# Norms 0, 2 and 3 of a hybrid decoder trunk: an earlier residual add on VectorE and a new order on ScalarE

## The chip, the cores and the metric

The kernel runs on one core of one Trainium2 chip. The metric is the device time of one execution in microseconds (us), the median of three runs. The engines are TensorE (PE, with its weight loads PEld), VectorE (DVE), ScalarE (ACT), GpSimd (POOL) and SyncE (SP), which issues the loads of the weights.

## The reference, cut to what matters

Two layers; each has four sublayers, and each sublayer ends in a layer norm of a residual sum. Everything is fp32.

```python
for l in range(DEPTH):
    x = layer_norm(ALPHA * x + 0.5 * swiglu(x, ffn1_w_in[l], ffn1_w_out[l]), ln1_g[l], ln1_b[l])
    x = layer_norm(ALPHA * x + mix, ln2_g[l], ln2_b[l])               # mix: RG-LRU, GLA, conformer
    x = layer_norm(ALPHA * x + memory_cross_attn(...), ln3_g[l], ln3_b[l])
    x = layer_norm(ALPHA * x + 0.5 * swiglu(x, ffn2_w_in[l], ffn2_w_out[l]), ln4_g[l], ln4_b[l])

def layer_norm(x, g, b):
    mu = jnp.mean(xf, axis=-1, keepdims=True)
    var = jnp.mean(jnp.square(xf - mu), axis=-1, keepdims=True)
    y = (xf - mu) * lax.rsqrt(var + EPS)
    return (y * g + b).astype(x.dtype)
```

The norms are numbered 0 to 3 in the kernel.

## The kernel before, in words

`x` lies in SBUF as 128 partitions by 8 feature tiles (`k` or `m`) by 512 positions. Every product is made of three passes: an operand is split into a high part (fp32r) and a low part, and TensorE adds high by high, high by low and low by high. Weights come as "slots" through a ring of four buffers `raw`; ScalarE copies a slot into one of two buffers `w_hi` (`w_hi_of`, L1272), GpSimd subtracts to get `w_lo` (`split`, L567), and TensorE multiplies. `w_hi_of(n)` waits until slot n-2 has been multiplied, since it overwrites that slot's buffer.

Norms 0, 2 and 3 work by halves of the positions, `h` = 0 (positions 0 to 255) and `h` = 1. For one of them the work goes as follows; `next_s` is the first slot of the next stage, `a` the first half, `b` the second:

- TensorE finishes the last output tile (norm 0, 3) or the last two (norm 2) for half `a`, then for half `b`. DVE adds the residual of half `a` (`half_added`, L1778), and later that of half `b` (`added_b`, which waits for TensorE's slot and calls `half_added` once for norm 0 and 3, twice for norm 2).
- TensorE sums over the features with a matrix of 1/1024 (L809: `stats_first`, `stats_rest`). ACT squares the mean (`square_of_mean`, L1312), DVE makes the variance (`variance`, L1784 and L1786), ACT its reciprocal root (`root`, L1316), and DVE refines the root (`scale`, L1792 to L1796).
- DVE centres `x` two tiles at a time (`centered_pair`, L1820), scales them (`normed_pair`, L1826) and in half 1, for `k` = 4 and 6, also applies gain and bias (`affine_pair`, two instructions L1832, SBUF to SBUF). For all other pairs ACT applies gain and bias (`affines`, L1322). ACT copies each pair to its high part (`copied`, L1366), and GpSimd makes its low part (`split_x`, L575).
- Meanwhile TensorE does not wait for the norm: `raw_pair` (L751, L753, L756) multiplies slots `next_s` and `next_s`+1 with the un-normed sums (made by ACT at L1294 and DVE at L1752), and a correction is applied afterwards (`sums_of` on ACT, L1371 to L1373). The sum over half `b` for the statistics (`stats_rest(…, 1)`) stands inside the first of these products, behind `k` = 5 (norm 0, 3) or `k` = 7 (norm 2). Then `second_pair` (L777, L783, L790) multiplies slot `next_s`+2 with the normed `x`, half by half: it waits for `w_hi`, for `sums_of(0)`, for each pair's high part, for `w_lo` and for each pair's low part.

All queues run in the order in which the code issues; there is no scheduler. GpSimd's order at a norm (`after_norm`) is: split of slots `next_s` and `next_s`+1, four `split_x` of half 0, split of slot `next_s`+2, four `split_x` of half 1, split of slot `next_s`+3. Norm 1 is not by halves, and norm 3 of the last layer takes other functions (`scaled_by_halves`) and keeps its order, so five norms are touched: norm 0, 2, 3 of layer 0 and norm 0, 2 of layer 1.

Of the kernel before, what the change touches and what calls it, by code (L numbers as in the profile page):

```python
# [65 lines left out]
def slot_width(s):  # L66

    if S_OUT[0] <= s < S_MIX or s >= S_OUT[1]:
        return FT // 2 * P
    if S_MIX + V_SLOT <= s < S_MIX + V_SLOT + 2:  # L70
        return 4 * W_B
    return KT * P
# [32 lines left out]
def group(layer, n, h):  # L105
    return layer * GROUPS + G_BASE[n] + h + 1
# [7 lines left out]
def later(layer, n):  # L114

    return n in RAW_NORMS and (layer, n) != (LAYERS - 1, 3)
# [19 lines left out]
def raw_bank(n, j, h):  # L136
    return 2 * (1 - j if n == 2 else j) + h
# [18 lines left out]
def x_count(layer, n, k, h=0):  # L156
    return KT + layer * XS + X_BASE[n] + h * KT + k + 1
# [47 lines left out]
def raw_count(n):  # L205

    return 16 * sum(pieces(i % SLOTS) for i in range(n % RAW, n + 1, RAW))
# [22 lines left out]
def hybrid_decoder(nc, x_in, mem_in, consts_in, vecs_in, mats_in, w_in1, w_out1, w_in2, w_out2,  # L230
                   w_mix, w_v, w_mixout, w_kv, w_q, w_o, out):
    ctx = ExitStack()
    with ctx:
# [77 lines left out]
        def tokens_in(n, h):  # L311
            return HALVES[h] if BY_HALVES[n] else slice(0, SEQ)

        def mean_of(n, h):
            return psum[:, 6 + h, HALVES[0]] if BY_HALVES[n] else bank(6)
# [7 lines left out]
        def first_root_of(n, h):  # L323
            return psum[:, 4 + h, HALVES[1]] if BY_HALVES[n] else bank(4)
# [931 lines left out]
        def _(act):  # L1256
# [8 lines left out]
            def w_hi_of(n):  # L1265

                if n >= SPLIT:
                    act.wait_ge(slot_multiplied, n - SPLIT + 1)
                if n < TOTAL:
                    act.wait_ge(raw_loaded[n % RAW], raw_count(n))  # L1270
                    width = slot_width(n % SLOTS)
                    A(w_hi[:, n % SPLIT, 0:width], raw[:, n % RAW, 0:width],  # L1272
                      ACT.Copy).then_inc(w_hi_made, 1)
# [33 lines left out]
            def silu_table():  # L1307
                A(small[:, 46:47], small[:, 47:48], ACT.Silu)

            def square_of_mean(layer, n, h):  # L1310
                act.wait_ge(stats_ready, group(layer, n, h))
                A(var[:, tokens_in(n, h)], mean_of(n, h), ACT.Square).then_inc(mean_squared, 1)  # L1312

            def root(layer, n, h):
                act.wait_ge(var_ready, group(layer, n, h))
                A(first_root_of(n, h), var[:, tokens_in(n, h)],  # L1316
                  ACT.Abs_reciprocal_sqrt).then_inc(root_ready, 1)

            def affine(layer, n, k, cols):
                act.wait_ge(y_centered, x_count(layer, n, k, 1 if cols.start else 0) - KT)  # L1320
                c = V_LN + 16 * n + k
                return A(x[:, k, cols], x[:, k, cols], ACT.Identity, bias=vec(c + 8), scale=vec(c))  # L1322
# [33 lines left out]
            def scaled_later(layer, n, next_s, square_b, to):  # L1356

                hi = NORMED[n][0]

                def affines(h, k):  # L1360
                    affine(layer, n, k, HALVES[h])
                    affine(layer, n, k + 1, HALVES[h])

                def copied(h, k):
                    cols = HALVES[h]
                    A(hi[:, k:k + 2, cols], x[:, k:k + 2, cols], ACT.Copy).then_inc(x_hi_made, 2)  # L1366

                def sums_of(j):
                    act.wait_ge(slot_multiplied, next_s + j + 1)
                    o = to(j)  # L1370
                    A(sums[:, 2 * j:2 * j + 2], psum[:, raw_bank(n, j, 1), HALF:HALF + 2], ACT.Copy)  # L1371
                    A(o[:, HALVES[0]], psum[:, raw_bank(n, j, 0), HALVES[0]], ACT.Copy)
                    A(o[:, HALVES[1]], psum[:, raw_bank(n, j, 1), HALVES[0]],  # L1373
                      ACT.Copy).then_inc(raw_sums_read, 1)

                square_of_mean(layer, n, 0)
                if n == 2:
                    w_hi_of(next_s)
                root(layer, n, 0)
                if n != 2:  # L1380
                    w_hi_of(next_s)
                affines(0, 0)
                affines(0, 2)
                square_b()
                w_hi_of(next_s + 1)
                if n != 2:
                    act.wait_ge(slot_multiplied, next_s)
                act.drain()
                copied(0, 0)
                copied(0, 2)  # L1390
                square_of_mean(layer, n, 1)
                affines(0, 4)
                root(layer, n, 1)
                affines(0, 6)
                act.drain()
                copied(0, 4)
                copied(0, 6)
                for k in range(0, KT, 2):
                    if k < 4:
                        affines(1, k)  # L1400
                        act.drain()
                    else:
                        act.wait_ge(y_centered, x_count(layer, n, k + 1, 1) - KT)
                    copied(1, k)
                    if k == 0:
                        sums_of(0)
                        w_hi_of(next_s + 2)
                    if k == 4:
                        w_hi_of(next_s + 3)
                sums_of(1)  # L1410
                silu_table()
# [311 lines left out]
        def _(dve):  # L1723
# [19 lines left out]
            def raw_lo(layer, n, m, h, cols):  # L1743

                c = V_LN + 16 * n
                z_hi, z_lo = RAW_Z[n]
                dve.wait_ge(raw_hi_made, raw_part(layer, n, m, h))
                if m == 0:
                    V.tensor_tensor(z_lo[:, :, SEQ:ROW],
                                    vecs[:, c:c + 2 * KT].rearrange("p (w k) -> p k w", w=2),  # L1750
                                    z_hi[:, :, SEQ:ROW].bitcast(F32), ALU.subtract)
                V.scalar_tensor_tensor(z_lo[:, m, cols], x[:, m, cols], vec(c + m),  # L1752
                                       z_hi[:, m, cols].bitcast(F32), ALU.mult,
                                       ALU.subtract).then_inc(raw_lo_made, 1)
# [26 lines left out]
            def variance(layer, n, h, eps):  # L1781

                v = var[:, tokens_in(n, h)]
                V.tensor_tensor(v, square_mean_of(n, h), v, ALU.subtract)  # L1784
                dve.drain()
                V.tensor_scalar(v, v, 0.0, eps, ALU.max, ALU.add).then_inc(var_ready, 1)  # L1786

            def scale(layer, n, h):

                v, r0 = var[:, tokens_in(n, h)], first_root_of(n, h)  # L1790
                dve.wait_ge(root_ready, group(layer, n, h))
                V.scalar_tensor_tensor(v, v, -0.5, r0, ALU.mult, ALU.mult)  # L1792
                dve.drain()
                V.tensor_tensor(v, v, r0, ALU.mult)
                dve.drain()
                V.scalar_tensor_tensor(scale_of(n, h), v, 1.5, r0, ALU.add, ALU.mult)  # L1796
# [20 lines left out]
            def centered_pair(n, h, k):  # L1817
                cols = HALVES[h]
                m = mean_of(n, h).rearrange("p (a s) -> p a s", a=1).to_broadcast([P, 2, HALF])
                V.tensor_tensor(x[:, k:k + 2, cols], x[:, k:k + 2, cols], m, ALU.subtract)  # L1820
# [15 lines left out]
            def norm_by_halves(layer, n, eps, added_b):  # L1836

                for h in range(2):
                    if h:
                        added_b()  # L1840
                    if later(layer, n):
                        for m in range(WHOLE[n], KT):
                            raw_lo(layer, n, m, h, HALVES[h])
                    dve.wait_ge(mean_squared, group(layer, n, h))
                    variance(layer, n, h, eps)
                    centered_pair(n, h, 0)
                    centered_pair(n, h, 2)
                    scale(layer, n, h)
                    normed_pair(n, h, 0).then_inc(y_centered, 2)
                    normed_pair(n, h, 2).then_inc(y_centered, 2)  # L1850
                    for k in range(4, KT, 2):
                        centered_pair(n, h, k)
                        last = normed_pair(n, h, k)
                        if h and later(layer, n):
                            last = affine_pair(n, h, k)
                        last.then_inc(y_centered, 2)
# [464 lines left out]
```

## Time and profile before

| what | value |
|---|---|
| runs (us) | 2215.99, 2216.14, 2215.76; median 2215.99 |
| profiled execution | 2216.65 us, span 2214.9 us |
| PE busy | 2171.3 us (98%) |
| PEld busy | 1814.8 us (82%) |
| DVE busy | 1119.5 us (51%) |
| ACT busy | 824.0 us (37%) |
| POOL busy | 990.5 us (45%) |
| mean granted TensorE clock | 0.997 |

Busy times are of the profiled execution; its own time is 1.75 us above its span, and 0.66 us above the median. Matmuls are pipelined, so a row of PE overlaps the next one: one 256-column matmul is listed with about 0.28 us, and the next starts 0.12 us after it. Below, a time such as 383.60 is us from the start of the span. A row of the timeline gives start, length, engine, line, operation, output and inputs with shape, the count of merged instructions, and in brackets the idle time of the engine before it and what ended that.

### The profile page before, as it was taken

Reading aid. Unit: us, or ns where it says so; the run is one execution under the profiler, and the core shown is the slowest. Engines: PE = TensorE matmul, PEld = TensorE weight load, DVE = VectorE, ACT = ScalarE, POOL = GpSimd, SP = SyncE. Lnnn points to the kernel's source line nnn. Section 1 sums busy time; section 2 is a strip of 40 time slices with the busy share of each in tenths; the row PEclk is TensorE's granted clock in tenths of the full one; section 3 lists DMA queues with packets and bytes.
Section 4 is the critical chain, followed back from the end, with each engine's and each line's share of the span. In section 5 each row is a group of like instructions: output and inputs, shape, how many; then the busy total and the mean of one; then the engine's idle time right before and its main releaser. Section 6 shows DMA issues by size and latency. Waiting matters only on the chain. (4 is left out here: it accounts for less than half of the span.)

```text
span 2214.9 us, 26968 instructions
## 1 busy us (share of the span) xinstructions
PE 2171.3 (98%) x11052; PEld 1814.8 (82%) x11052; DVE 1119.5 (51%) x1222; ACT 824.0 (37%) x1148; POOL 990.5 (45%) x408
## 2 busy tenths in 40 slices
PE   8999999999999999999999999999999999999997
PEld 7888889788778888888888888898786888888886
DVE  4433235987746733323454333369877376333234
ACT  3322224836444522222353222257355344222223
POOL 3444444436443544444354444454265335444442
PEclk9999999999999999999999999999999999999999
DMA  5333322333332233332233333223243222333321
GB/s 179 96 95 95 114 100 62 89 103 105 107 93 67 77 95 96 96 120 92 74 105 95 95 99 117 89 67 86 90 121 113 77 67 80 101 96 95 114 94 49
DMA packets 96043, 210.91 MB, mean 95 GB/s; under 512 B 39344, under 2 KB 52016, under 8 KB 95664
## 3 DMA queue, kind: packets, MB, share of 16 engines
q1 hardware_dynamic: 94944, 208.19, 30.4%
q8 instruction: 87, 1.43, 0.3%
q10 hardware_dynamic: 976, 1.00, 0.1%
q14 instruction: 36, 0.29, 0.0%
HBM read 207.06 MB, written 2.10 MB: 94 GB/s over the span
## 5 line engine op out<-in xcount | busy, mean ns | idle before, releaser
L567 POOL TENSOR_TENSOR w_lo<-raw,w_hi 128x1024 fp32r<-128x1024 f32 (+2 forms) x358 | 930.9, 2602 | 1197.0 <-ACT w_hi L1272 1196.9
L1272 ACT ACTIVATE w_hi<-raw 128x1024 fp32r<-128x1024 f32 (+2 forms) x358 | 401.6, 1122 | 1217.8 <-PE psum L647 1141.1
L641 PE MATMUL psum<-acts_hi,w_hi 128*128 128x512 f32 x1744 | 685.1, 393 | 3.4 <-ACT tmp L1648 3.0
L644 PE MATMUL psum<-acts_lo,w_hi 128*128 128x512 f32 x1744 | 679.8, 390 | 0.0
L647 PE MATMUL psum<-acts_hi,w_lo 128*128 128x512 f32 x1744 | 430.8, 389 | 0.0
L641 PEld LDWEIGHTS psum<-acts_hi,w_hi 128*128 128x128 f32 x1744 | 328.0, 188 | 76.5 <-issue 3.9
L644 PEld LDWEIGHTS psum<-acts_lo,w_hi 128*128 128x128 f32 x1744 | 328.0, 188 | 69.7 <-issue 2.4
L647 PEld LDWEIGHTS psum<-acts_hi,w_lo 128*128 128x128 f32 x1744 | 327.4, 188 | 68.0
L1885 DVE TENSOR_TENSOR work<-work,psum 128x512 f32<-128x512 f32 x85 | 58.5, 688 | 548.8 <-PE psum L647 542.0
L641 PE MATMUL psum<-h_hi,w_hi 128*128 128x512 f32 x616 | 239.6, 389 | 0.0
L644 PE MATMUL psum<-h_lo,w_hi 128*128 128x512 f32 x616 | 239.6, 389 | 0.0
L1890 DVE TENSOR_TENSOR h_lo<-work,h_hi 128x512 fp32r<-128x512 f32 x88 | 231.2, 2628 | 6.6
L1766 DVE SCALAR_TENSOR_TENSOR x<-x,psum 128x512 f32<-128x512 f32 x56 | 38.4, 686 | 283.9 <-PE psum L647 283.4
L647 PE MATMUL psum<-h_hi,w_lo 128*128 128x512 f32 x616 | 148.7, 389 | 0.0
L1773 DVE TENSOR_TENSOR work<-work 128x512 f32<-128x512 f32 x54 | 138.2, 2559 | 14.5 <-ACT work L1302 12.7
L644 PEld LDWEIGHTS psum<-h_lo,w_hi 128*128 128x128 f32 x616 | 115.6, 188 | 24.0
L641 PEld LDWEIGHTS psum<-h_hi,w_hi 128*128 128x128 f32 x616 | 115.6, 188 | 24.0
L647 PEld LDWEIGHTS psum<-h_hi,w_lo 128*128 128x128 f32 x616 | 115.6, 188 | 24.0
L1969 DVE SCALAR_TENSOR_TENSOR psum<-tmp,vecs,psum 128x512 f32<-128x512 f32 x116 | 87.6, 755 | 9.2 <-issue 0.4
L1302 ACT ACTIVATE work<-x 128x512 f32<-128x512 f32 (+1 forms) x72 | 41.1, 571 | 61.4 <-DVE x L1778 41.2
L1322 ACT ACTIVATE x<-x,vecs 128x256 f32<-128x256 f32 (+1 forms) x92 | 53.5, 630 | 19.5 <-DVE x L1826 14.4
L1771 DVE TENSOR_TENSOR work<-work,x 128x512 f32<-128x512 f32 x54 | 52.1, 964 | 5.3 <-issue 0.4
(300 smaller groups left out, 2484.6 us busy)
## 6 DMA issues: line engine op xcount, KB each, us to landing
raw<-w_in SPq DMA_DIRECT2D x176, 512.0 KB, 3.6
raw<-w_out SPq DMA_DIRECT2D x64, 704.0 KB, 4.0
raw<-w_kv SPq DMA_DIRECT2D x32, 512.0 KB, 3.6
raw<-w_mix SPq DMA_DIRECT2D x26, 512.0 KB, 3.6
raw<-w_q SPq DMA_DIRECT2D x16, 512.0 KB, 3.6
raw<-w_o SPq DMA_DIRECT2D x16, 512.0 KB, 3.6
raw<-w_v SPq DMA_DIRECT2D x4, 768.0 KB, 4.2
raw<-w_mix SPq DMA_DIRECT2D x24, 128.0 KB, 3.3
```

Of the source, the lines that this page charges most:

```text
L567: nc.gpsimd.tensor_tensor(w_lo[:, n % SPLIT, 0:width], raw[:, n % RAW, 0:width], w_hi[:, n % SPLIT, 0:width].bitcast(F32), ALU.subtract).t ...
L641: nc.tensor.matmul(o, hi, b_hi, start=start and k == 0, stop=False)
L644: nc.tensor.matmul(o, hi, b_lo, start=False, stop=False)
L647: last = nc.tensor.matmul(o, weight(r, k)[1], operand(k)[0], start=False, stop=stop and k == n - 1)
L1272: A(w_hi[:, n % SPLIT, 0:width], raw[:, n % RAW, 0:width], ACT.Copy).then_inc(w_hi_made, 1)
L1302: A(zsq(m)[:, cols], x[:, m, cols], ACT.Square).then_inc(z_squared, 1)
L1322: return A(x[:, k, cols], x[:, k, cols], ACT.Identity, bias=vec(c + 8), scale=vec(c))
L1771: V.tensor_tensor(zsum, zsum, x[:, m, :], ALU.add)
L1773: V.tensor_tensor(zsqsum, zsqsum, zsq(m), ALU.add).then_inc(z_summed, 1)
L1885: V.tensor_tensor(h, work[:, i % 2, :], bank(hidden_bank(layer, f, i, 1)), ALU.mult).then_inc(h_made, 1)
L1890: V.tensor_tensor(lo, h, hi.bitcast(F32), ALU.subtract).then_inc(h_split, 1)
L1969: V.scalar_tensor_tensor(total, u_pad[:, t, j:j + SEQ], w, total, ALU.mult, ALU.add)
```

## The change

In `norm_by_halves` (DVE) `added_b` moves from the start of half 1 into half 0: in norm 2 ahead of the pair `k` = 4, in norms 0 and 3 ahead of the pair `k` = 6. In `scaled_later` (ACT) `square_of_mean` of half 1 moves ahead of the first two copies of half 0, `root` of half 1 ahead of `affines(0, 4)`, and `w_hi_of(next_s + 2)` from behind `sums_of(0)` to ahead of the loop over half 1.

```diff
@@ scaled_later, ScalarE
                 square_b()
                 w_hi_of(next_s + 1)
+                square_of_mean(layer, n, 1)
                 if n != 2:
                     act.wait_ge(slot_multiplied, next_s)
                 act.drain()
                 copied(0, 0)
                 copied(0, 2)
-                square_of_mean(layer, n, 1)
+                root(layer, n, 1)
                 affines(0, 4)
-                root(layer, n, 1)
                 affines(0, 6)
                 act.drain()
                 copied(0, 4)
                 copied(0, 6)
+                w_hi_of(next_s + 2)
                 for k in range(0, KT, 2):
...
                     if k == 0:
                         sums_of(0)
-                        w_hi_of(next_s + 2)
@@ norm_by_halves, VectorE
                 for h in range(2):
-                    if h:
+                    if h and not later(layer, n):
                         added_b()
...
                     for k in range(4, KT, 2):
+                        if h == 0 and later(layer, n) and k == (4 if n == 2 else 6):
+                            added_b()
                         centered_pair(n, h, k)
```

VectorE's queue in norm 2 of layer 0, from the scaling of the first two pairs of half 0, before:

```order
L1826 TENSOR_TENSOR x<-x,psum 128x2x256 x2
L1820 TENSOR_TENSOR x<-x,psum 128x2x256
L1826 TENSOR_TENSOR x<-x,psum 128x2x256
L1820 TENSOR_TENSOR x<-x,psum 128x2x256
L1826 TENSOR_TENSOR x<-x,psum 128x2x256
L1778 SCALAR_TENSOR_TENSOR x<-x,psum 128x256 x2
L1752 SCALAR_TENSOR_TENSOR z_lo<-x,vecs,z_hi 128x256 x2
L1784 TENSOR_TENSOR var<-psum,var 128x256
```

And the same stretch after the change:

```order
L1826 TENSOR_TENSOR x<-x,psum 128x2x256 x2
L1778 SCALAR_TENSOR_TENSOR x<-x,psum 128x256 x2
L1820 TENSOR_TENSOR x<-x,psum 128x2x256
L1826 TENSOR_TENSOR x<-x,psum 128x2x256
L1820 TENSOR_TENSOR x<-x,psum 128x2x256
L1826 TENSOR_TENSOR x<-x,psum 128x2x256
L1752 SCALAR_TENSOR_TENSOR z_lo<-x,vecs,z_hi 128x256 x2
L1784 TENSOR_TENSOR var<-psum,var 128x256
```

The two residual adds (L1778) stand four instructions earlier; in norms 0 and 3 the one add stands two earlier, ahead of the last L1820 and L1826 of half 0.

ScalarE's queue in norm 0 of layer 0, as the difference from the copy of slot `next_s`+1 on (L1272 is a weight copy, L1312 the squared mean, L1316 the root, L1322 gain and bias, L1366 a copy to the high part):

```order
 L1272 ACTIVATE w_hi<-raw 128x1024
+L1312 ACTIVATE var<-psum 128x256
 L1366 ACTIVATE x_hi<-x 128x2x256 x2
-L1312 ACTIVATE var<-psum 128x256
-L1322 ACTIVATE x<-x,vecs 128x256 x2
-L1316 ACTIVATE psum<-var 128x256
-L1322 ACTIVATE x<-x,vecs 128x256 x2
+L1316 ACTIVATE psum<-var 128x256
+L1322 ACTIVATE x<-x,vecs 128x256 x4
 L1366 ACTIVATE x_hi<-x 128x2x256 x2
+L1272 ACTIVATE w_hi<-raw 128x1024
 L1322 ACTIVATE x<-x,vecs 128x256 x2
```

The squared mean now stands ahead of two copies, the root ahead of all four gains of `k` = 4 to 7, and the third weight copy ahead of half 1's first gains. TensorE's queue, GpSimd's and SyncE's are as before.

## Rows read from the trace of the kernel before

**Rows 1.** Who TensorE waited for: us in total, times, longest us (whole run)
```profile
PE psum L809 <- DVE x L1778: 2.7, 3, 1.1
PE psum L790 <- POOL x_lo L575: 2.6, 3, 0.9
```

**Rows 2.** TensorE's timeline, norm 0 of layer 0: its last two waits
```profile
389.49 0.50 PE L777 MATMUL psum<-x_hi,w_hi 128*128 128x256 f32 x2 [0.24 <-ACT x_hi L1366]
...
392.59 0.50 PE L790 MATMUL psum<-x_lo,w_hi 128*128 128x256 f32 x2 [0.92 <-POOL x_lo L575]
```

**Rows 3.** TensorE's timeline, norm 2 of layer 0
```profile
732.27 1.12 PE L1227 MATMUL psum<-q_hi,w_lo 128*128 128x256 f32 x8
...
737.48 1.13 PE L809 MATMUL psum<-x,consts 128*128 128x256 f32 x4 [1.05 <-DVE x L1778]
...
748.97 1.22 PE L777 MATMUL psum<-acts_hi,w_hi 128*128 128x256 f32 x8 [0.78 <-ACT w_hi L1272]
...
753.62 0.50 PE L777 MATMUL psum<-acts_hi,w_hi 128*128 128x256 f32 x2 [0.24 <-ACT acts_hi L1366]
...
756.52 0.50 PE L790 MATMUL psum<-acts_lo,w_hi 128*128 128x256 f32 x2 [0.73 <-POOL acts_lo L575]
```

**Rows 4.** TensorE's timeline, norm 0 of layer 0: last slot of the stage
```profile
371.44 1.67 PE L888 MATMUL psum<-h_hi,w_lo 128*128 128x256 f32 x11
```

**Rows 5.** VectorE's timeline, norm 0 of layer 0
```profile
373.25 0.41 DVE L1778 SCALAR_TENSOR_TENSOR x<-x,psum 128x256 f32<-128x256 f32 x1
...
377.51 0.58 DVE L1786 TENSOR_SCALAR var<-var 128x256 f32<-128x256 f32 x1
...
383.60 0.73 DVE L1832 TENSOR_SCALAR x<-x,vecs 128x256 f32<-128x256 f32 x2
...
385.78 2.93 DVE L1832 TENSOR_SCALAR x<-x,vecs 128x256 f32<-128x256 f32 x2
```

**Rows 6.** ScalarE's timeline, norm 0 of layer 0
```profile
376.61 0.36 ACT L1312 ACTIVATE var<-psum 128x256 f32<-128x256 f32 x1
...
378.12 0.39 ACT L1316 ACTIVATE psum<-var 128x256 f32<-128x256 f32 x1 [0.17 <-DVE var L1786]
...
379.60 1.15 ACT L1366 ACTIVATE x_hi<-x 128x512 fp32r<-128x512 f32 x2
...
383.69 1.07 ACT L1272 ACTIVATE w_hi<-raw 128x1024 fp32r<-128x1024 f32 x1
...
388.80 0.63 ACT L1366 ACTIVATE x_hi<-x 128x512 fp32r<-128x512 f32 x1 [0.89 <-DVE x L1832]
```

**Rows 7.** GpSimd's timeline, norm 0 of layer 0
```profile
375.55 2.39 POOL L567 TENSOR_TENSOR w_lo<-raw,w_hi 128x1024 fp32r<-128x1024 f32 x1 [3.69 <-ACT w_hi L1272]
377.90 5.11 POOL L575 TENSOR_TENSOR x_lo<-x,x_hi 128x512 fp32r<-128x512 f32 x4
384.85 2.41 POOL L567 TENSOR_TENSOR w_lo<-raw,w_hi 128x1024 fp32r<-128x1024 f32 x1 [1.83 <-ACT w_hi L1272]
387.21 5.33 POOL L575 TENSOR_TENSOR x_lo<-x,x_hi 128x512 fp32r<-128x512 f32 x4
```

**Rows 8.** Timelines of VectorE, ScalarE and GpSimd, norm 2 of layer 0
```profile
732.57 1.47 DVE L1826 TENSOR_TENSOR x<-x,psum 128x512 f32<-128x512 f32 x2
...
741.63 0.61 DVE L1786 TENSOR_SCALAR var<-var 128x256 f32<-128x256 f32 x1
...
733.29 2.09 ACT L1322 ACTIVATE x<-x,vecs 128x256 f32<-128x256 f32 x4 [2.27 <-DVE x L1826]
737.13 0.42 ACT L1302 ACTIVATE work<-x 128x256 f32<-128x256 f32 x1 [1.75 <-DVE x L1778]
...
739.67 2.42 POOL L567 TENSOR_TENSOR w_lo<-raw,w_hi 128x1024 fp32r<-128x1024 f32 x1 [6.43 <-ACT w_hi L1272]
```

**Rows 9.** L1752 on VectorE over the run: duration ns min/median/max
```profile
L1752 DVE SCALAR_TENSOR_TENSOR z_lo<-x,vecs,z_hi x20: 484/739/2877, 701.9 to 1836.8; 128x512 fp32r<-128x512 f32 x12, 128x256 fp32r<-128x256 f32 x8
```

**Rows 10.** VectorE's timeline in the mixer of layer 0: its slack against TensorE
```profile
474.91 1.38 DVE L2024 COPY_PREDICATED work<-consts,psum 128x1024 f32<-128x1024 uint32 x1 [2.54 <-PE psum L988]
```

## The prediction

> **What bounds the kernel now.** I read the page's busy times first: TensorE is busy 98% of the span at a granted clock of 0.997, so the time can fall only where TensorE waits, and rises only where it waits more. The list of TensorE's waits comes next. The waits of the touched norms are small: three times for the residual add at the statistics (two of them, 1.05 us each, in norm 2), three times for GpSimd's low part of `x` in norms 0 and 3 [rows 1, 3]. Then the timelines of the engines in one norm 0 and one norm 2; layer 1 and norm 3 repeat them within 0.3 us. In norm 0 TensorE waits 0.24 us for the high part of the last pair and 0.92 us for its low part [rows 2]. In norm 2 it waits 1.05 us at the statistics, 0.78 us for the third weight copy, and 0.24 and 0.73 us for the last pair [rows 3]. All of it together, over five norms, is under 10 us; it is the most that there is to win.
>
> The reader should see one more thing, the length of VectorE's L1832 (gain and bias). The pair of `k` = 4 takes 0.73 us while GpSimd is idle; the pair of `k` = 6 takes 2.93 us while GpSimd works without a gap [rows 5, 7]. Its two instructions end about 0.15 us after an instruction of GpSimd each: the split ends at 387.26, the first low part at about 388.55, and the pair ends at 388.71. L1786 does the same: reached at 377.51, it ends at 378.09, 0.15 us after GpSimd's split (377.94). So such an instruction waits for the GpSimd instruction that is running, and the next for the one after it. The Trainium skill says this as a rule (SBUF — State Buffer, Who interferes with whom): a `tensor_scalar` in a 2-port mode and a GpSimd instruction exclude each other for a whole instruction. The trace agrees (0.73 against 2.93 us).
>
> **Norms 0 and 3 (three of them).** The times are of norm 0 in layer 0.
> - The earlier add. TensorE's last slot ends at 371.44 + 1.67 = 373.11 [rows 4], and the add started at 373.25 [rows 5]. It can win 0.14 us at most; I take 0.08. VectorE stands still for it from 371.9, then does `k` = 6 of half 0; that was idle time before, and ACT wants that pair only at 378. Cost nothing.
> - Squared mean. The statistics stand at a fixed place in TensorE's queue, done at 376.1. ACT squares at 376.17, not 376.61 [rows 6]. VectorE reaches L1786 about 0.5 us earlier, but GpSimd's split runs till 377.94 - 0.08 [rows 7], so the variance ends at 378.01 instead of 378.09, and the root starts at 378.04 instead of 378.12. The new place of `square_of_mean` buys 0.08 us.
> - Root ahead of four gains. Four L1322 take 2.1 us behind the root where two did. The copies of `k` = 4 and 6 start at 380.51 instead of 379.60, 0.9 us later. GpSimd's third low part starts at 381.22; with 1.25 to 1.3 us each (5.11 for four) the fourth ends at 383.78, not 383.01.
> - Third weight copy. It follows the copies, at 381.57 to 382.64 instead of from 383.69: 2.1 us earlier. GpSimd's split runs at 383.73 to 386.13 instead of 384.85 to 387.26, 1.1 us earlier, and its idle time of 1.83 us [rows 7] is gone.
> - What is late next. The pair `k` = 4 of half 1 lay in that idle time. Now VectorE reaches it at 383.55, GpSimd is busy till 383.78, the first instruction ends at 383.93, and the second waits for the whole split, till 386.28 (before 384.33). The pair `k` = 6 comes 1.44 us later (385.78 - 384.33, about), at 387.72; its instructions end behind the second and third low part, at 388.87 and 390.15, instead of 388.71. ACT's copy takes 0.09 + 0.63 us, so TensorE gets the last pair at 390.93 instead of 389.49. From there to the last low part it has 14 matmuls at 0.12 us and a restart, 2.01 us: 392.94 instead of 392.59. GpSimd has its low part by 392.3; that wait is gone. Per norm **+0.35 us**.
>
> Bounds: were VectorE never held, the last pair would stay at 389.49 and TensorE would end at 391.50, -1.1 us. If VectorE reached `k` = 4 just after GpSimd began the split (0.2 us decide), both its instructions wait, the pair ends at 387.75, and `k` = 6 at 390.65: +0.85 us. A further low part of 1.3 us is the far end, +1.3 us in all; more is not to be had, because GpSimd itself starves without the last pair and lets VectorE in. I take +0.35, since 383.55 lies before 383.73. Sum of three: +1.05.
>
> **Norm 2 (two of them).** The times are of layer 0.
> - The earlier add wins much here: TensorE's slots are done at 733.39 [rows 3], VectorE is free at 733.96 (rows 8: 732.57 + 1.47, overlapping a little). The statistics follow TensorE's product with no wait at 736.17 instead of 737.48, -1.31 us for TensorE at that point.
> - ACT's squares start right behind its four gains (733.29 + 2.09), at 735.28 instead of 737.13, and with them the second weight copy and GpSimd's split, which started at 739.67 [rows 8]: -1.85 us, so 737.82 to 740.24.
> - VectorE does its two L1752 behind `k` = 6 now: the second starts at 733.96 + 2 x 0.33 + 2 x 1.36 + 0.4 = 737.74. It reads two operands from SBUF, and the long ones of this line (2877 ns against 739) [rows 9] wait, as I read it, for GpSimd too. It is 0.08 us ahead of GpSimd. If it is first, GpSimd starts at 738.2, ends at 740.60, the variance ends at 740.75 instead of 742.24 (741.63 + 0.61 in rows 8): -1.49 us.
> - From there the chain of norm 0: `k` = 4 is reached 5.51 us behind the variance (378.09 to 383.60), at 746.26; ACT's copies let GpSimd's fourth low part end at 746.52 and the split at 748.87; VectorE ends `k` = 4 at 749.02, `k` = 6 at 752.90. TensorE gets the last pair at 753.68 (before 753.62) and ends at 755.69 instead of 756.52. The waits at the statistics and for the weight copy go, but most of it comes back as a longer wait for the last pair. Per norm **-0.83 us**.
>
> Bounds: with the affine pair never held, GpSimd's chain sets the end, at about 754.0 (-2.5 us), and without any hold of the variance either, -3.6 us. On the other side stands the second rival below, +0.07 us. Sum of two: -1.66.
>
> **Downstream.** VectorE leaves norm 0 at 390.15 instead of 388.71. Two L2079 follow that waited for GpSimd before and will wait less, and in the mixer VectorE still has 2.54 us in hand where TensorE keeps it waiting [rows 10]. I count nothing.
>
> **Sum.** 2216.65 (the profiled execution: span 2214.90 and 1.75 around it) + 1.05 - 1.66 = 2216.04. The profiled run was 0.66 above the median, so **2215.4** against 2215.99.
>
> **Rivals.** Within 0.2% (4.4 us) a measurement of this kernel can't tell from no change.
> - *L1752 loses in norm 2.* GpSimd starts first by a few hundredths; the second L1752 waits till 740.24, the variance then stands behind the first low part and ends at 741.65. The last pair comes at 754.58, TensorE ends at 756.59, +0.07. For it: the margin is 0.08 us. Against: the estimate has VectorE first. With +1.05 of the other norms: 2217.2. The same page of the Trainium skill (SBUF — State Buffer, Who interferes with whom) has a DVE instruction with two SBUF inputs contend with a GpSimd one that reads SBUF, whoever is first; rows 9 fit, but no row shows this pair of instructions.
> - *VectorE is hardly held.* If the instructions slip in between GpSimd's, the work won on ACT arrives: three times -1.1, twice -2.5: -8.3, 2207.7. Against it speaks the pair `k` = 6, held twice in a row (2.93 us) [rows 5], in every norm alike.
> - *Slower: VectorE carries its delay into the mixer.* The pair `k` = 4 misses the gap ahead of the split, +0.85 in three norms; VectorE leaves norm 0 at 390.65, 1.94 us late, and TensorE waits for it in both mixers. 2.55 + 3.9 + 0.15 = +6.6: 2222.6. It decides from the point where the delay exceeds the 2.54 us [rows 10]; it would need 0.6 us more of contention.
> - *Nothing moves.* The add in norm 2 gets no earlier, say for its slot: 2216.0. Against: 733.39 is before 733.96.
>
> **How the numbers follow.** Forecast 0.63 (its own range 2213.8 to 2216.9), L1752 loses 0.17, hardly held 0.09, carried into the mixer 0.05, nothing moves 0.06. The range 2212.3 to 2217.9 takes in the second, the last and a part of the faster case (holds of half the length). Faster by over 0.2% needs -4.4 us: the third case and a tail of the forecast, 0.10. Slower: 0.05. No change: 0.85.
>
> **What would show it.** In norm 0: L1832 of `k` = 4 near 2.7 us instead of 0.73; L1786 ending within 0.1 us of its old time; GpSimd without its idle 1.83 us; TensorE's wait for `x_hi` near 1.7 us instead of 0.24, and none for `x_lo`. In norm 2: no wait at L809, the wait for `x_hi` the largest, near 2 us. Wrong if L1832 of `k` = 4 stays short, or if TensorE ends a norm over 1 us off these times.

## The result: slower by 0.3%, though the last high part came within 0.1 us of the forecast

| | before | after |
|---|---|---|
| median of 9 runs (us) | 2216.14 (2215.76 to 2216.74) | 2222.80 (2220.17 to 2224.84) |
| profiled execution, span | 2216.65, 2214.9 | 2224.84, 2223.1 |
| mean granted TensorE clock | 0.997 | 0.993 |

The ratio is 1.0029, 95% interval 1.002 to 1.0037. The change costs 6.7 us where the prediction had -0.6 us, and the time lies outside its range. The nine runs of the changed kernel spread over 4.7 us, those of before over 1.0 us; that spread is itself part of the answer.

The profile after, who TensorE waited for (us in total, times, longest), against [rows 1]:

```profile
PE psum L777 <- ACT x_hi L1366: 5.6, 3, 1.9
PE psum L777 <- ACT acts_hi L1366: 4.6, 2, 2.4
PE psum L777 <- issue: 1.6, 2, 0.8
PE psum L809 <- DVE x L1778: 0.6, 1, 0.6
```

The waits for GpSimd's low parts are gone, so is that of 1.05 us at norm 2's statistics. In their place stand five long waits for the last high part, 10.2 us together. The two of 0.8 us put down to "issue" are those ahead of the third slot in norm 2, which the prediction had as waits for the weight copy and expected to go: the copy is no longer late, but TensorE stands as long as before. They cost nothing at the end of the norm, since the last pair comes later still.

TensorE's timeline after, norm 0 of layer 0, against [rows 2]:

```profile
388.52 0.88 PE L777 MATMUL psum<-x_hi,w_hi 128*128 128x256 f32 x6
391.27 0.50 PE L777 MATMUL psum<-x_hi,w_hi 128*128 128x256 f32 x2 [1.87 <-ACT x_hi L1366]
391.61 1.79 PE L783 MATMUL psum<-x_hi,w_lo 128*128 128x256 f32 x8
393.20 1.91 PE L790 MATMUL psum<-x_lo,w_hi 128*128 128x256 f32 x8
394.90 0.51 PE L641 MATMUL psum<-x_hi,w_hi 128*128 128x512 f32 x1
```

The stage reaches this norm 0.28 us later than before (the three timelines start apart by that much), so 391.27 answers to a forecast of 390.93 + 0.28 = 391.21, and the wait of 1.87 us to a forecast near 1.7. What follows it was not forecast: eight matmuls of L790 take 1.91 us, where they take 1.12 at full clock. The granted clock is in the column PEclk, here for four stretches of the changed kernel (start and end in us, length, then busy time of PE, PEld, DVE, ACT, POOL with instructions, PEclk, DMA share, GB/s): the two at the waits of norm 0 and norm 2 in layer 0, and what follows each.

```profile
391.75:395.15 3.40, 3.40 (x18) 3.40 (x17) 3.07 (x6) 3.37 (x6) 3.40 (x2) 0.50 0.00 0
395.16:400.00 4.84, 4.84 (x22) 4.00 (x22) 4.37 (x7) 4.84 (x7) 1.85 (x2) 1.00 0.34 108
756.98:760.38 3.40, 3.36 (x15) 3.36 (x16) 2.92 (x6) 2.69 (x6) 3.27 (x2) 0.50 0.00 0
760.39:765.00 4.61, 4.61 (x23) 3.88 (x23) 2.01 (x3) 1.55 (x2) 3.06 (x2) 1.00 0.42 114
```

And the first of these stretches in the kernel before:

```profile
391.75:395.15 3.40, 2.56 (x12) 2.19 (x13) 3.25 (x3) 2.58 (x3) 3.15 (x2) 1.00 0.00 0
```

TensorE is busy through the whole 3.40 us in the changed kernel, at half the clock, 1.2 GHz instead of 2.4. Around all five touched norms the changed kernel has such a stretch, the kernel before has none (a wider view over each norm of the changed kernel):

```profile
386.00:396.00 10.00, 8.13 (x52) 7.76 (x51) 9.28 (x16) 7.65 (x13) 8.16 (x6) 0.83 0.17 52
752.00:766.00 14.00, 11.86 (x67) 10.73 (x66) 9.69 (x14) 6.98 (x12) 10.44 (x7) 0.88 0.27 77
1120.00:1131.00 11.00, 9.11 (x54) 8.46 (x54) 9.68 (x14) 7.62 (x13) 8.79 (x7) 0.84 0.29 71
1488.00:1499.00 11.00, 9.13 (x55) 8.38 (x54) 10.16 (x17) 8.71 (x14) 7.93 (x6) 0.84 0.27 67
1855.00:1866.00 11.00, 8.56 (x48) 7.89 (x48) 8.90 (x13) 6.13 (x11) 8.30 (x6) 0.84 0.29 92
```

What one such stretch costs can be read from the rows above. From the last pair's start to the next slot's first matmul it is 394.90 - 391.27 = 3.63 us; the same 18 matmuls at full clock take 0.34 + 16 x 0.12 = 2.26 us. That is 1.37 us, and the stretch lasts 0.25 us longer.

The touched norms are not the only place. Once per layer TensorE also waits 1.5 us for ScalarE in the attention stage (L641, for a tile made at L1648), which no version here touches. At this wait the clock fell once in the kernel before, in layer 1, and twice in the changed kernel, in both layers. Before, layer 1, the wait and its stretch; then the changed kernel, layer 0:

```profile
1711.86 0.63 PE L641 MATMUL psum<-acts_hi,w_hi 128*128 128x512 f32 x1 [1.49 <-ACT tmp L1648]
1712.08:1715.48 3.40, 3.40 (x9) 2.62 (x9) 2.13 (x2) 1.16 (x2) 3.40 (x2) 0.50 0.18 55
```
```profile
617.50 0.79 PE L641 MATMUL psum<-acts_hi,w_hi 128*128 128x512 f32 x1 [1.49 <-ACT tmp L1648]
617.03:620.43 3.40, 2.92 (x7) 2.35 (x8) 1.51 (x1) 1.86 (x3) 3.38 (x2) 0.50 0.22 84
```

Both kernels have the same 11052 matmuls in the same order, so their starts can be subtracted one by one. The table has what TensorE lost against the kernel before from ahead of each norm to 20 matmuls into the slot behind it, in us of the profiled executions. "Filled" is an experiment of the next section, the changed kernel without the falls behind these waits.

| norm, layer | forecast | changed | filled |
|---|---|---|---|
| 0, 0 | +0.35 | +1.81 | +0.33 |
| 2, 0 | -0.83 | +0.45 | -0.99 |
| 3, 0 | +0.35 | +1.78 | +0.25 |
| 0, 1 | +0.35 | +1.84 | +0.35 |
| 2, 1 | -0.83 | +0.75 | -0.71 |
| sum | -0.61 | +6.63 | -0.77 |

Changed less filled is 1.4 to 1.5 us in each of the five. The 6.6 us of the norms, 1.3 us lost in the attention stage of layer 0 and 0.3 us ahead of the first norm make up the 8.2 us between the two profiled executions.

The hold of VectorE came as forecast. Its timeline after, norm 0 of layer 0, against [rows 5]:

```profile
377.37 0.90 DVE L1786 TENSOR_SCALAR var<-var 128x256 f32<-128x256 f32 x1
...
383.78 2.88 DVE L1832 TENSOR_SCALAR x<-x,vecs 128x256 f32<-128x256 f32 x2
...
388.09 2.40 DVE L1832 TENSOR_SCALAR x<-x,vecs 128x256 f32<-128x256 f32 x2
```

L1786 is reached 0.4 us earlier and ends at 378.27, only 0.10 us earlier than before (378.09 + 0.28 at that point), since it is held longer. The pair of `k` = 4 takes 2.88 us where it took 0.73, because GpSimd's third split now follows its low parts at once:

```profile
381.54 2.56 POOL L575 TENSOR_TENSOR x_lo<-x,x_hi 128x512 fp32r<-128x512 f32 x2 [0.85 <-ACT x_hi L1366]
384.04 2.47 POOL L567 TENSOR_TENSOR w_lo<-raw,w_hi 128x1024 fp32r<-128x1024 f32 x1
```

### The profile page after: what moved, and what is told of

Its sections match the earlier page's. It is cut to its first block and busy times, and to the rows that moved or that the text cites. A ratio compares the mean times of both kernels' runs of the same rounds, so it can differ in the third digit from the quotient of the medians.

```text
span 2223.1 us, 26968 instructions
## 1 busy us (share of the span) xinstructions
PE 2177.3 (98%) x11052; PEld 1822.3 (82%) x11052; DVE 1116.5 (50%) x1222; ACT 824.4 (37%) x1148; POOL 991.5 (45%) x408
## 5 line engine op out<-in xcount | busy, mean ns | idle before, releaser
L1272 ACT ACTIVATE w_hi<-raw 128x1024 fp32r<-128x1024 f32 (+2 forms) x358 | 401.5, 1121 | 1222.2 <-PE psum L647 1144.4
L641 PE MATMUL psum<-acts_hi,w_hi 128*128 128x512 f32 x1744 | 685.9, 393 | 3.5 <-ACT tmp L1648 3.0
L641 PEld LDWEIGHTS psum<-acts_hi,w_hi 128*128 128x128 f32 x1744 | 328.5, 188 | 76.7 <-issue 3.9
L641 PE MATMUL psum<-h_hi,w_hi 128*128 128x512 f32 x616 | 239.6, 389 | 0.0
L641 PEld LDWEIGHTS psum<-h_hi,w_hi 128*128 128x128 f32 x616 | 115.6, 188 | 24.0
L1322 ACT ACTIVATE x<-x,vecs 128x256 f32<-128x256 f32 (+1 forms) x92 | 53.0, 628 | 16.2 <-DVE x L1826 11.1
```

The lines of the kernel that those rows point to most:

```text
L641: nc.tensor.matmul(o, hi, b_hi, start=start and k == 0, stop=False)
L1272: A(w_hi[:, n % SPLIT, 0:width], raw[:, n % RAW, 0:width], ACT.Copy).then_inc(w_hi_made, 1)
```

## The experiments

Two questions: which part of the change does the harm, and is it the order of the engines or the clock. The code shown is an extract of each edit; the comments in it are for the reader. "Before" was run beside each; the ratios are against it.

**VectorE's part alone** (`added_b` as in the change, ScalarE's queue untouched).

> VectorE's part of the change alone (ScalarE's queue as before). Theory (the loss comes from ScalarE's new order, which takes GpSimd's idle gap away from VectorE's gain-and-bias pair and so makes one long wait of TensorE for the last pair's high part, behind which its clock falls): the gap is still there, so L1832 of k = 4 stays at 0.7 us and the wait for the last high part at 0.2 to 0.5 us; no fall of the clock behind a norm; in norm 2 the wait at L809 goes and the whole chain is about 1.85 us earlier, so about -3.7 us for two norms: 2212.4. Rival (the earlier residual add does the harm, VectorE standing still for it): about 2222.

Measured: 2211.47 us, ratio 0.9982 (0.9973 to 0.9991), 11 runs. The earlier add is the good half of the change. In norm 2 TensorE's wait at the statistics is gone, and the wait for the last high part is as before:

```profile
736.12 1.02 PE L809 MATMUL psum<-x,consts 128*128 128x256 f32 x4
...
751.88 0.51 PE L777 MATMUL psum<-acts_hi,w_hi 128*128 128x256 f32 x2 [0.24 <-ACT acts_hi L1366]
...
754.78 0.50 PE L790 MATMUL psum<-acts_lo,w_hi 128*128 128x256 f32 x2 [0.73 <-POOL acts_lo L575]
```

The last row stood at 756.52 [rows 3]: 1.74 us earlier, of which 0.15 us was there ahead of this norm. Subtracted as in the table above, the two norms 2 give -1.6 us each and the other three -0.1 each, -3.5 in all; the profiled execution also has no fall of the clock in the attention stage, where that of the kernel before has one. The rival is out.

**ScalarE's part alone** (VectorE's queue untouched).

> ScalarE's part of the change alone (VectorE's queue as before). Theory: waits for the last high part of 1.6 to 2 us in all five norms, L1832 of k = 4 near 2.8 us, mechanical cost about +0.35 three times and +0.55 twice (+2.1), and a stretch at the lower clock behind most of these waits at 1.3 us each: 2222 to 2226. Rival (the earlier add does the harm): 2216, no wait over 0.5 us.

Measured: 2223.61 us, ratio 1.0035 (1.0023 to 1.0048), 5 runs. The harm is ScalarE's. Its waits for the last high part are about those of the changed kernel (5.9 us in three, 4.6 in two). In the profiled execution the clock fell behind two of the five norms only, so "most" was too much; it fell in both attention stages as well. The three norms without a fall lost 0.43 us (norm 0) and 0.57 and 0.84 us (norm 2), so about 2.7 us of the five is order and not clock.

**The wait filled with work.** The changed kernel with 12 more matmuls ahead of the last high part's wait:

```diff
                     for k in range(KT):
+                        if h == 1 and k == KT - 2:
+                            for i in range(12):
+                                nc.tensor.matmul(outs[1][:, cols], weight(ring(layer, s), i % 4)[0],
+                                                 x_hi[:, i % 4, cols], start=i == 0, stop=i == 11)
```

> The changed kernel, and in second_pair 12 more matmuls of 256 columns into the bank of the next slot (which that slot overwrites) ahead of the wait for the last high part of half 1: they fill 1.44 us of that wait with TensorE work and change no result. Theory clock: the granted clock stays at 2.4 GHz behind the norms, the time falls to what the engines' order alone gives, 2215 to 2217.5, though TensorE does 60 matmuls more. Rival (order alone made it 6.7 us slower, the clock is a bystander): the fill is hidden in the wait and the time stays at 2222 to 2224.

Measured: 2215.59 us (2214.84 to 2217.90), ratio 0.9999 (0.9991 to 1.0008), 11 runs. Sixty useless matmuls make the changed kernel 7.2 us faster. The waits shrink to 0.5 us (norms 0 and 3) and 1.0 us at most (norm 2), and the clock stays whole in all five norms; the first and the second:

```profile
386.00:396.00 10.00, 9.54 (x70) 8.89 (x69) 9.28 (x16) 7.62 (x13) 8.14 (x6) 1.00 0.18 52
748.00:762.00 14.00, 13.09 (x85) 11.95 (x86) 12.91 (x14) 7.92 (x15) 11.73 (x7) 1.00 0.24 79
```

Nothing but TensorE's activity in the wait differs, so the loss is the clock's. What is left is what the engines' order gives. The median lies 0.6 us under that of before, but the interval of the ratio reaches from -2.0 to +1.8 us; the table above is sharper, -0.77 us in five norms against the -0.61 of the prediction. Against VectorE's part alone (-3.5 us in the five norms) ScalarE's part costs 2.7 us by order, and 7.4 more by the clock (the sums of "changed" and "filled").

**The wait made longer in the kernel before.** ScalarE copies something useless ahead of its last high part, two or three times:

```diff
+                    if k == 6:
+                        for i in range(3):                     # 2 in the other
+                            A(work[:, 1, :], x[:, 0, :], ACT.Copy)
+                            act.drain()
                     copied(1, k)
```

> The kernel before, with three extra copies of 512 columns on ScalarE (into an unused part of work) ahead of its copy of the last high part of half 1 in the five norms: about 1.7 us later, nothing else touched. Theory clock: TensorE's wait for that part goes from 0.24 us to about 1.9 us (2.2 in norm 2); by the order alone this costs 0.6 us three times and 0.8 to 1.2 twice, +3.8: 2220; with stretches at 1.2 GHz behind most of the waits it is 2224 to 2227. Rival (no clock, only the order): 2220, no lower clock behind the norms.

> As late3 with two extra copies (about 1.15 us): the wait becomes about 1.4 us. By the order alone +1.0: 2217.2. If a wait of this length is enough for the clock to fall, 2221 to 2224; if it needs a longer one, 2217. I hold the second for likelier, since single waits of 1.3 and 1.5 us later in the run are mostly not followed by a fall.

Measured: with three 2226.50 us, ratio 1.0045 (1.0032 to 1.0058), 5 runs; with two 2218.05, ratio 1.0008 (0.9999 to 1.0017), 11 runs. Norm 0 of layer 0 with two copies and with three:

```profile
389.89 0.51 PE L777 MATMUL psum<-x_hi,w_hi 128*128 128x256 f32 x2 [1.59 <-ACT x_hi L1366]
```
```profile
390.94 0.50 PE L777 MATMUL psum<-x_hi,w_hi 128*128 128x256 f32 x2 [2.28 <-ACT x_hi L1366]
```

Waits of 1.6 us, five of them, were followed by no fall in the profiled execution, and cost 2.1 us. That is not a safe length: in the same execution the clock fell behind both waits of 1.5 us in the attention stages. Waits of 2.3 us, 0.7 us longer each, cost 10.5: 8.4 us more where the lengths account for 3.4. In the profiled execution with three copies the clock fell behind three norms. These lost 2.3 to 2.6 us each, the two without a fall 0.85 and 1.04. Norm 3 of layer 0:

```profile
1122.00:1133.00 11.00, 8.72 (x46) 7.69 (x45) 8.33 (x10) 9.49 (x16) 9.38 (x6) 0.84 0.41 111
```

**ScalarE's part split.** The squared mean and the root alone, and the third weight copy alone.

> Of ScalarE's part only the squared mean and the root in their new places; the third weight copy stays behind sums_of(0), VectorE's queue as before. GpSimd keeps an idle gap of about 1.2 us ahead of its third split, the pair k = 4 of half 1 ends about 0.25 us later; the wait for the last high part is about 0.45 us. Order alone +0.2 us in five norms, no fall of the clock: 2217. If the roots' new place is what makes the long wait: over 2221.

> Of ScalarE's part only the third weight copy in its new place. GpSimd's idle gap goes, the pair k = 4 of half 1 is held twice (about 3.2 us instead of 0.73), the pair k = 6 is held once; the last high part comes about 1.0 us later, the wait for it is about 1.3 us (late2: about 1.4 us, few falls of the clock). Order alone 0 to +0.1 per norm: 2216 to 2217.5. If the wait comes to 1.8 us or more, the clock falls and it is 2221 to 2225.

Measured: 2217.22 us, ratio 1.0007 (0.9998 to 1.0016), and 2216.09 us, ratio 1.0000 (0.9992 to 1.0009), 11 runs each. With the weight copy alone the pair `k` = 4 is held twice, as expected:

```profile
383.47 3.23 DVE L1832 TENSOR_SCALAR x<-x,vecs 128x256 f32<-128x256 f32 x2
...
388.13 1.44 DVE L1832 TENSOR_SCALAR x<-x,vecs 128x256 f32<-128x256 f32 x2
```

and the waits are 1.35 us in norms 0 and 3, as forecast, but 2.3 to 2.6 us in norm 2, where I had 1.3. None was followed by a fall in the profiled execution, which is the fastest of the eleven (2214.37 us, mean granted clock 0.998); the slowest took 2218.41 us at 0.996, so falls did come in some runs, though no trace of them says where. Norm 2 of layer 0:

```profile
754.23 0.50 PE L777 MATMUL psum<-acts_hi,w_hi 128*128 128x256 f32 x2 [2.34 <-ACT acts_hi L1366]
```

Neither part alone is slow. Together, in norms 0 and 3, they add: the roots' new place makes GpSimd's low parts of half 0 late by 0.9 us, the weight copy takes the gap away, and the wait goes from 1.35 to 1.87 us. In norm 2 they do not: the wait is no longer with both (2.14 and 2.44 us) than with the weight copy alone, and why the clock spared it there is not shown.

**A new order on TensorE.** In `second_pair`, half 1:

```diff
-                for h in range(2):
-                    hi_by_hi(h)
...
+                hi_hi(1, 0, KT - 2)
+                lo_hi(1, 0, KT - 2)
+                hi_lo(1, 0, 4)
+                hi_hi(1, KT - 2, KT)      # waits for the last high part
+                lo_hi(1, KT - 2, KT)
+                hi_ready(layer, s + 1)
+                for k in range(KT):       # next slot, high by high
+                    nc.tensor.matmul(outs[1], weight(r, k)[0], x_hi[:, k, :],
+                                     start=k == 0, stop=False)
+                hi_lo(1, 4, KT).then_inc(slot_multiplied, 1)
```

> The changed kernel with second_pair's half 1 in another order on TensorE: low by high of k = 0 to 5 and high by low of k = 0 to 3 ahead of the wait for the last high part, and the eight high by high passes of the next slot ahead of the last low parts. Same arithmetic. Theory: TensorE has 1.2 us of work for the wait for the high part and 1.8 us for the one for the low part; no wait over 1.2 us, no fall of the clock behind norms 0 and 3, and -0.6 us three times, -1.9 twice against the kernel before: 2210.5. Rival (order alone, no clock): not under 2216.

> The kernel before with TensorE's new order alone. -1.1 to -1.5 three times, -1.0 twice: 2210.3. If GpSimd's low parts set the end anyway: 2216.

> VectorE's part of the change alone, with TensorE's new order of second_pair: the version I expect to beat both. Norms 0 and 3: the waits for the last high and low part go, -1.1 to -1.5 us each; norm 2: about -2.8 each. Sum -9 to -10: 2206.6. Rival (the two gains are the same one, since GpSimd's low parts set the end in both): no better than VectorE's part alone, 2211.5.

Measured: on the changed kernel 2210.46 us, ratio 0.9974 (0.9965 to 0.9984), 10 runs; on the kernel before 2209.51, ratio 0.9971 (0.996 to 0.9982), 7 runs; with VectorE's part alone **2205.23 us**, ratio 0.9953 (0.994 to 0.9965), 5 runs, 10.7 us below before and the fastest of all. Its wait list has one line left of those in [rows 1 to 3] and above:

```profile
PE psum L777 <- ACT w_hi L1287: 1.1, 2, 0.6
```

The two gains, -4.7 and -6.5 us, add up almost whole (-10.7): they lie in different waits. All three forecasts held within 1.4 us.

## Why the prediction was wrong

**The step that failed** is the last of each norm's chain: "From there to the last low part it has 14 matmuls at 0.12 us and a restart, 2.01 us", and the same 2.01 us in norm 2. It prices the longer wait for the last pair by its length and takes the clock behind it for a constant, read once as 0.997 at the top and never asked about again. The chain up to the wait was right, and so were its sums by order (+0.33 and -0.99 us measured in the first norms 0 and 2, against +0.35 and -0.83). What was put at nothing is the clock: behind each of the five waits TensorE ran 3.4 us at 1.2 GHz, 1.4 to 1.5 us lost each time, 7.4 us in all. So TensorE left each of the five norms 1.3 to 1.6 us later than the forecast, more than the 1 us that the prediction gave as a sign of being wrong. No rival had it. The number that came near, 2222.6, belonged to another mechanism, and its own working does not hold: a delay of 1.94 us fits into the 2.54 us that VectorE has in hand [rows 10], so TensorE would have waited for none of it.

**Point by point:**
- *VectorE held by GpSimd.* Right: 2.8 to 2.9 us for `k` = 4 against about 2.7, in every touched norm.
- *Squared mean buys nothing.* Right in norm 0: L1786 ended 0.10 us earlier, forecast 0.08.
- *The last pair's time.* Right in norm 0 (391.27 against 391.21). In norm 2 as well: the whole norm ran 3.44 us later than before (its two adds at 737.40 against the forecast 733.96, after falls of the clock further up), so the forecast is 753.68 + 3.44 = 757.12, and the trace after has

```profile
740.78 0.88 DVE L1752 SCALAR_TENSOR_TENSOR z_lo<-x,vecs,z_hi 128x256 fp32r<-128x256 f32 x2
...
757.02 0.80 PE L777 MATMUL psum<-acts_hi,w_hi 128*128 128x256 f32 x2 [2.14 <-ACT acts_hi L1366]
```

- *L1752 first.* Right: its two instructions took 0.88 us, not held; the rival in which it loses is out.
- *The waits in norm 2.* That at the statistics went; that ahead of the third slot stayed (0.81 us, was 0.78), which cost nothing here. With the first, *nothing moves* is out.
- *The sum by order alone, -0.6 us.* Borne out by the table, -0.77 us in five norms. That the filled kernel's median is also 0.6 us lower (2215.59 against 2216.17) is within the noise.
- *Hardly held* (-8.3 us): out, L1832 was held throughout.
- *Slower, through the mixer:* wrong mechanism. VectorE's slack there is not used up, it grew from 2.54 us [rows 10] to 2.89:

```profile
477.01 1.38 DVE L2026 COPY_PREDICATED work<-consts,psum 128x1024 f32<-128x1024 uint32 x1 [2.89 <-PE psum L988]
```

**What stays open.** Not each long wait is followed by a fall: in the profiled executions it is five of five in the changed kernel (1.87 to 2.44 us), two of five with ScalarE's part alone (1.97 to 2.42), three of five with three extra copies (2.3 us), none of five with two extra copies (1.6 us) and none of five with the weight copy alone (1.35 to 2.6 us). Of the 1.5 us waits of the attention stage, two in each of the twelve profiled executions, 12 of 24 were. The length of the wait does not decide alone, and what does was not tried; nor is it shown that the fall in the attention stage of layer 0, which the profiled execution of the kernel before lacks, comes from the change. It makes the time scatter: single runs of the changed kernel lie anywhere from 2220.2 us (mean granted clock 0.995) to 2224.8 us (0.993), about three falls apart.

## What to carry to other kernels

A wait of TensorE is not priced by its length alone: several short waits merged into one long wait can cost more than their sum, because the clock may fall behind it. When a change moves waits, ask for the longest single one after it, not only for the total, and give TensorE work that it can do ahead of it (here 10 matmuls of the same slot ahead of the last high part, and 8 of the next slot ahead of the last low parts). Look at the granted clock of the kernel before as well: a mean of 0.997 hid one such fall. And an idle gap of GpSimd may be the place in which VectorE's SBUF-to-SBUF instructions get through; closing it is not free.

## What the runs showed of the hardware

- Around the end of some waits of 1.5 to 2.4 us TensorE's granted clock fell from 2.4 to 1.2 GHz for 3.4 us and then came back; behind the waits of the norms one fall cost 1.4 to 1.5 us, in the attention stage of layer 0 it cost 1.3. With 12 matmuls of no use in the wait none of the five came. The Trainium skill tells how waits bring TensorE back to the low clock again and again (TensorE: Matmul & The Clock Gate, HAM oscillation — how this bites in real kernels), there in loops that wait for a DMA, about 3 to 5 us, at each tile. The trace agrees that the clock falls at waits; these runs add that single waits of 1.5 us and more, in a run that is 98% busy, can be enough.
- Five waits of 1.6 us were not followed by a fall in the profiled execution, while both waits of 1.5 us in the same execution were.
- VectorE's `tensor_scalar` from SBUF to SBUF, 0.41 us for 256 columns when alone, took up to 2.50 us (longest single one, ScalarE's part alone) while GpSimd ran subtractions of 2.4 us.
